# A gated delta rule layer: rows of decays reach all partitions by loads from memory instead of by matrix products

## The reference

```
gc = cumsum(g)                      # log decays, per head, inside a chunk of 64
dmat[i, j] = exp(gc[i] - gc[j])     # for j <= i, else 0
a_mat = strict_lower((k * beta) k^T * dmat)
qk    = lower(q k^T * dmat)
sol   = solve(I + a_mat, [v * beta, k * beta * exp(gc)])
q_dec = q * exp(gc)                 # queries that read the state
```

## Time and profile before

| | us |
|---|---|
| median of 3 runs (lowest, highest) | 1590.81 (1590.49, 1592.78) |
| the profiled execution, its own time | 1594.32 |
| its span in the trace | 1592.6 |
| PE busy | 1563.1 (98%) |
| PE weight loads busy | 1481.5 (93%) |
| DVE busy | 1055.5 (66%) |
| ACT busy | 884.4 (56%) |
| POOL busy | 256.2 (16%) |

### The profile page before, as it was taken

The page is one execution under the profiler, slowest core; times in us unless marked ns, Lnnn a source line. Parts: engine busy times, 40 slices in busy tenths (PEclk is TensorE's granted clock), DMA queues, the critical chain, the costliest instruction groups (busy, mean ns, idle before and its releaser), DMA issues.

```text
span 1592.6 us, 37769 instructions
## 1 busy us (share of the span) xinstructions
PE 1563.1 (98%) x16212; PEld 1481.5 (93%) x16212; DVE 1055.5 (66%) x1732; ACT 884.4 (56%) x1696; POOL 256.2 (16%) x328
## 2 busy tenths in 40 slices
PE   9999999999999999999999999999999999999997
PEld 7998799999997999999788888999999997999997
DVE  7965686755757877547793747776469837767643
ACT  6856656633645666434652546665358547566433
POOL 7105450000110200003003421100010035400000
PEclk9999999999999999999999999999999999999999
DMA  8941456565753665653635003665569512565550
GB/s 244 292 140 29 134 164 179 183 206 175 255 160 133 200 176 185 195 185 94 189 96 144 20 7 98 176 185 186 186 182 261 174 55 82 165 181 184 188 167 28
DMA packets 245529, 250.10 MB, mean 157 GB/s; under 512 B 16270, under 2 KB 239284, under 8 KB 245300
## 3 DMA queue, kind: packets, MB, share of 16 engines
q1 hardware_dynamic: 237204, 224.78, 46.3%
q0 software_dynamic: 8016, 22.86, 4.9%
q10 hardware_dynamic: 144, 0.05, 0.0%
HBM read 229.75 MB, written 18.32 MB: 156 GB/s over the span
## 4 chain that ended last, share of the span: by engine, by line
PE 92%; ACT 4%; DVE 3%; issue 1%; DMA 0%; SPq 0%; DVEq 0%
PE ps L844 88%; PE ps L848 4%; ACT vk L2053 1%; ACT tri L2053 1%; ACT acts L2053 1%; ACT st L2053 0%; DVE acts L2760 0%; ACT hn L2053 0%; DVE tri L2752 0%; DVE acts L2752 0%; DMA acts<-in_x_sample_dram 0%; ACT L2056 0%; PE ps L1796 0%; DVE st L2760 0%; DVE hn L2760 0%
## 5 line engine op out<-in xcount | busy, mean ns | idle before, releaser
L2752 DVE TENSOR_TENSOR w_mlp<-ring,w_mlp 128x1024 fp32r<-128x1024 f32 x256 | 311.7, 1224 | 119.9 <-ACT w_mlp L2053 113.9
L2053 ACT ACTIVATE w_mlp<-ring 128x1024 fp32r<-128x1024 f32 x256 | 269.4, 1054 | 208.2 <-PE ps L844 208.2
L844 PE MATMUL ps<-hn_split,w_mlp 128*128 128x264 f32 x3072 | 373.3, 284 | 0.0
L844 PE MATMUL ps<-h_split,w_mlp 128*128 128x264 f32 x3072 | 372.6, 283 | 0.0
L844 PEld LDWEIGHTS ps<-hn_split,w_mlp 128*128 128x128 f32 x3072 | 372.0, 188 | 0.3
L844 PEld LDWEIGHTS ps<-h_split,w_mlp 128*128 128x128 f32 x3072 | 371.6, 188 | 0.0
L2053 ACT ACTIVATE tri<-ps 128x264 f32<-128x264 f32 (+4 forms) x222 | 101.4, 463 | 181.2 <-PE ps L844 156.2
L844 PE MATMUL ps<-gdn_hi,w_gdn 128*128 128x264 f32 x896 | 165.8, 285 | 0.0
L844 PEld LDWEIGHTS ps<-gdn_hi,w_gdn 128*128 128x128 f32 x896 | 139.3, 188 | 0.9 <-issue 0.8
L844 PE MATMUL ps<-mixer_lo,w_gdn 128*128 128x264 f32 x448 | 126.9, 283 | 0.0
L2752 DVE TENSOR_TENSOR tri<-tri 128x264 f32<-128x264 f32 (+4 forms) x145 | 59.7, 413 | 101.3 <-ACT h_split L2053 100.6
(11 more groups left out here) (454 smaller groups left out, 2654.2 us busy)
## 6 DMA issues: line engine op xcount, KB each, us to landing
ring<-in_ffn_w_dram SPq DMA_DIRECT2D x128, 1024.0 KB, 5.4
ring<-in_gdn_w_in_dram SPq DMA_DIRECT2D x32, 1024.0 KB, 8.3
ring<-in_ml_w_in_dram SPq DMA_DIRECT2D x12, 1024.0 KB, 5.5
ring<-in_rw_w_rkv_dram SPq DMA_DIRECT2D x12, 1024.0 KB, 5.0
st<-in_state_gdn_S_dram POOLq DMA_DIRECT2D x2, 4096.0 KB, 22.4
ring<-in_gdn_w_out_dram SPq DMA_DIRECT2D x8, 1024.0 KB, 5.0
out_gdn_S_s_dram<-st SPq DMA_DIRECT2D x16, 512.0 KB, 6.8
st<-in_state_mlstm_C_dram POOLq DMA_DIRECT2D x1, 4096.0 KB, 20.5
```

The costliest lines, as they stand in the source:

```text
L844: return nc.tensor.matmul(out, lhsT, rhs, start=start, stop=stop)
L2053: return nc.scalar.activation(out, in_, f, bias=bias, scale=scale)
L2752: return nc.vector.tensor_tensor(out, in0, in1, op)
```

## The change

The products that spread rows over partitions are gone from both delta layers: the 32 of `spread` and the 8 of `spread_queries`. In their place one product of 16 output rows (8 heads of query exponents, 8 heads of matrix exponents) and 256 columns is made at the start of `decay_exponents` into bank 4. ACT copies these 16 rows to SBUF twice, once as they are and once as exponentials, and starts five DMAs from its own queue that write them to two small arrays in the chip's memory: 4 for the two matrices and the two groups of heads (16 runs of 256 bytes each), 1 for the queries (8 KB). POOL waits for all five (`row_out`) and starts three loads from there, whose source repeats the same 8 KB for every partition: two of 64 partitions x 8 KB into `AT6` and `QK6` at once, one of 128 partitions x 8 KB into `QS`. DVE waits for all three (`spr_in`), adds `negC` to each matrix with one operation in SBUF, and ACT takes both exponentials one after the other at n == 30. The exponentials of the queries are taken on the 16 rows, so the four ACT operations of 128x512 on `QS` are gone. The buffer of sample states `statio` moves to other space, which makes POOL clear it and `vv` ahead of `rtx` rather than after. In the constants the columns of `selt` are renumbered.

```diff
@@ names and arrays
-        qe_mm = rt_mm
-        spread_mm = kk_mm
+        row_mm = rt_mm
+        row_ev = rt_ok
+        exp_rows = [nc.dram_tensor(f"exp_rows{n}", (2, 2, 4, 4, HD), F32, kind="Internal").ap() for n in range(2)]
+        query_rows = [nc.dram_tensor(f"query_rows{n}", (GH, SEQ), F32, kind="Internal").ap() for n in range(2)]
+        row_log, row_exp = rows[0:2 * GH, 3, 0:SEQ], rows[0:2 * GH, 4, 0:SEQ]
-        statio = A(6).rearrange("p a b -> p (a b)")[:, 0:D].rearrange("p (h s n) -> p h s n", h=GH, s=NS)
+        statio = acts[:, 56:64, :].rearrange("p a b -> p (a b)")[:, 0:D].rearrange("p (h s n) -> p h s n", h=GH, s=NS)
@@ PE, decay_exponents, query_exponents and the fills
-                    for half in range(2):
-                        spread(0, 4 + half, half)
+                    b = 4
+                    pe.wait_ge(*last_read[b])
+                    mm(ps[b][0:2 * GH, 0:SEQ], selt[:, 0:2, :].rearrange("p a h -> p (a h)"), RG[:, 0:SEQ]).then_inc(row_mm, count.up(row_mm))
+                    last_read[b] = row_ev, count.seen(row_ev)
...
                 def query_exponents():
-                    for half in range(2):
-                        spread(4, 4 + half, half)
                     gram(0, 7)
                     gram(1, 6)
...
-                def spread_queries():
-                    for q in range(4):
-                        b = 2 + q
-                        pe.wait_ge(*last_read[b])
-                        for n in range(2):
-                            last = mm(ps[b][:, n * SEQ:(n + 1) * SEQ], sel(4, 2 * q + n, P), RG[:, 0:SEQ])
-                        last.then_inc(qe_mm, count.up(qe_mm))
-                        last_read[b] = eq_ev, count.expect(eq_ev)
...
-                fills = {(0, 0): sample_products, (0, 1): spread_queries, (1, 0): sample_outputs,
+                fills = {(0, 0): sample_products, (1, 0): sample_outputs,
@@ ACT
                     if n == 27:
+                        ac.wait_ge(row_mm, count.seen(row_mm))
+                        act(row_log, ps[4][0:2 * GH, 0:SEQ], ACT.Copy)
+                        act(row_exp, ps[4][0:2 * GH, 0:SEQ], ACT.Exp).then_inc(row_ev, count.up(row_ev))
+                        ac.wait_ge(row_ev, count.own(row_ev))
+                        for q in range(2):
+                            for g in range(2):
+                                at = q * GH + 4 * g
+                                ac.dma_start(exp_rows[j][g, q].rearrange("c h i -> h c i"),
+                                             rows[at:at + 4, 3, 0:SEQ].rearrange("h (c i) -> h c i", c=4)).then_inc(
+                                                 row_out, count.up(row_out, 16))
+                        ac.dma_start(query_rows[j], rows[0:GH, 4, 0:SEQ]).then_inc(row_out, count.up(row_out, 16))
                         ac.wait_ge(cols_mm, count.seen(cols_mm))
...
-                    if n in (29, 30):
-                        ac.wait_ge(da_ok, count.seen(da_ok, 2))
-                        part = AT6 if n == 29 else QK6
-                        act(part, part, ACT.Exp).then_inc(dt_ok, count.up(dt_ok))
+                    if n == 30:
+                        for part in (AT6, QK6):
+                            ac.wait_ge(da_ok, count.seen(da_ok))
+                            act(part, part, ACT.Exp).then_inc(dt_ok, count.up(dt_ok))
...
-                for q in range(4):
-                    ac.wait_ge(qe_mm, count.seen(qe_mm))
-                    act(QS[:, 2 * q:2 * q + 2, :], ps[2 + q][:].rearrange("p (n t) -> p n t", n=2), ACT.Exp).then_inc(
-                        eq_ev, count.up(eq_ev))
@@ DVE
-                dv.wait_ge(negc_ok, count.seen(negc_ok))
-                exponents(AT6, 4, 0)
-                exponents(AT6, 5, 1)
                 weight_lo()
+                dv.wait_ge(rtx_ok, count.seen(rtx_ok))
                 dv.wait_ge(cols_ok, count.seen(cols_ok))
...
-                exponents(QK6, 4, 0)
-                exponents(QK6, 5, 1)
+                dv.wait_ge(negc_ok, count.seen(negc_ok))
+                dv.wait_ge(spr_in, count.seen(spr_in, 48))
+                for part in (AT6, QK6):
+                    tt(part, part, negC, ALU.add).then_inc(da_ok, count.up(da_ok))
@@ POOL
-                gp_.tensor_tensor(hs8(rtx), bc(RG[:, SEQ:T], GH, 1), bc(mh[:], NS, 2), ALU.mult).then_inc(rtx_ok, count.up(rtx_ok))
                 gp_.memset(statio, 0.0)
                 gp_.memset(vv, 0.0)
+                gp_.tensor_tensor(hs8(rtx), bc(RG[:, SEQ:T], GH, 1), bc(mh[:], NS, 2), ALU.mult).then_inc(rtx_ok, count.up(rtx_ok))
+                count.seen(row_ev)
+                po.wait_ge(row_out, 80 * (j + 1))
+                for g, r in enumerate(halves):
+                    load(A(5).rearrange("p a b -> p (a b)")[r, 0:2 * D], bc(exp_rows[j][g].rearrange("s c h i -> (s c h i)"), HD, 0), spr_in)
+                load(QS.rearrange("p h t -> p (h t)"), bc(query_rows[j].rearrange("h t -> (h t)"), P, 0), spr_in)
                 po.wait_ge(cols_ok, count.seen(cols_ok))
...
-                        po.wait_ge(eq_ev, count.seen(eq_ev))
+                        if l == 1:
+                            po.wait_ge(spr_in, 48 * (j + 1))
```

26 lines of the change are left out of this document (6 added, 20 removed).

## The result

| | before | changed |
|---|---|---|
| median (lowest to highest) of 6 runs each, us | 1590.65 (1589.84 to 1593.66) | 1602.78 (1600.42 to 1608.86) |
| profiled execution, its span | 1594.32, 1592.6 | 1600.94, 1599.2 |

The changed kernel is slower: ratio 1.0078, 95% interval 1.0057 to 1.0099. That is 12.1 us in the medians and 6.6 in the two profiled executions. It lies 3.8 above the predicted range, on the side of the rival *the rows are back late*.

What follows compares the result with a forecast made beforehand. PE, busy 92% of the span, was taken to bound the kernel. Per layer +0.35 before level 0, -1.45 after it and +1.3 for the clock made +0.2, +0.4 in both: 1591.2 us, range 1584.5 to 1599.

Steps and rivals of the forecast that it cites:

- the rows are back late: Rival: rows land at 129, level 0 starts at 135.3, time 1596.6; chance 0.35 for late or more clock lost.
- landed to level 0: DVE's two adds, ACT's second exponential, Gram multiplications, a POOL mask and hand-overs before level 0: 6.3 us.
- PE's list: PE's products per delta layer: 7.25 us removed, 0.46 added, so 6.8 us go.
- ACT's copies and issues: After the row product: two copies of 0.3 to 0.45 us, five DMA issues of 0.4 each, last starting at 114.9.
- The store must land: From ACT's last issue until POOL goes on: 2.5 us, at 117.4 (116.2 to 119.3).
- The loads: Three loads of 2.1 MB ahead of level 0: 9.4 us (8.4 to 11.4), landed at 126.8.
- After level 0: Levels 1 and 2 of the solve: of 3.65 us removed, 1.45 remain per layer (bounds 2.8 and 0.7).
- the bank's wait: Level 1, half 0 waits for the bank that DVE reads, leaving 2.8 of 3.65 us.
- the masks beside `mvs`: POOL's level 2 masks meet DVE's masked values and run longer, giving back 1.35 us (0 to 2.1).
- The clock: PE's idle time of 3.3 us ahead of level 0 brings a clock fall: 1.3 us per layer (0 to 2.5).
- The sum: Both layers +0.4 us on the profiled 1594.32, less 3.5 for the median: 1591.2 (1581.5 best, 1602.9 worst).

Runs made afterwards that it cites:

- load_waits: Full change, but SP issues the next block's first weight load only when the three loads of the rows have landed; 1593.68 us, ratio 1.0015.
- split_and_waits: Full change, but DVE waits for the matrices' two loads alone and SP holds the next block's first weight load until these landed; 1586.23 us, ratio 0.9974.
- the second comparison: The full change run once more, unaltered, with a second profile, against the kernel before; 1600.96 us, ratio 1.0057.
- keep_busy: Full change plus eleven products that nobody reads on PE ahead of level 0; 1597.60 us, ratio 1.0042.
- with the masks ahead: Full change, DVE waiting for the matrices' loads alone, weight load held, POOL's masks ahead of the previous level's products; 1583.98 us, ratio 0.9953.
- split_wait: Full change, but DVE waits for the matrices' two loads alone and POOL waits for the query rows at level 1; 1594.21 us, ratio 1.0017.
- all_three: Full change with the matrices' loads made one onto 128 partitions, query rows awaited at level 1, weight load held; 1622.10 us, ratio 1.0198.
- queries_only: Kernel before, with only the query rows sent through memory and the matrices' products kept; 1593.44 us, ratio 1.0002.

## Why the prediction was wrong

In us, first layer:

| step | forecast | full change, first layer | without what lay across it |
|---|---|---|---|
| row product to last issue | 3.8 | 3.36 | 3.35 (load_waits) |
| last issue to landed | 2.5 (1.8 to 3.7 from rows) | 5.30 | 1.63 (load_waits) |
| loads landed | 9.4 (8.4 to 11.4) | 10.83 | 7.1 (split_and_waits, for the two that DVE needs) |
| landed to level 0 | 6.3 | 6.25 | 6.25 (load_waits) |
| in all | 22.0 | 25.74 | |

- *PE's list* (6.8 us gone, PE ready 18.7 after the row product): right. PE was through 18.73 after it.
- *ACT's copies and issues*, *landing to level 0*: right, to 0.4 and 0.05.
- *The store must land, 2.5*: the step that failed. It measured 5.30 and 5.27 in the two layers, outside its bounds of 1.8 to 3.7. It was sized from the medians of the earlier trace rows, without a look at what was in the queues beside them. For a store with nothing beside it 2.5 was even too much (1.63). The weight load that now comes at the same time was seen, and was put down as an argument for the late rival, with the answer that it is over before the big loads start. That is true and beside the point: it lies across the store, and everything behind waits for the last of five stores. 2.8 us.
- *The loads, 9.4*: 10.83 and 9.35 in the first profile, 10.99 and 10.82 in the second, so too small by 1.4 to 1.6 in three of four. The half rate on half the partitions, which the rule of the Trainium skill said (SBUF — State Buffer, section on the DMA port swizzle) and no row showed, is shown now. But what made 7.1 into 10.8 is DVE's wait for the query rows, which are not needed there. With the weight load away the three loads still took 9.61 and 11.19 (`load_waits`); why they vary stays open. The late rival named this place.
- *After level 0, 1.45 gained*: right, 1.65 (the bank's wait 0.99 for 0.85, the masks beside `mvs` as said). The order of POOL that avoids it was not thought of.
- *The clock, 1.3 with bounds 0 and 2.5*: mis-sized. In the four solves of the two profiles it cost 1.5, 1.5, 2.9 and 4.9 behind level 0; the last had a second fall, at 1326 to 1334. The price of one fall, 1.6, had been read right from the earlier trace rows; wrong was to count on less than one for each layer.
- *The sum*: the profile of before (1594.32) had falls of its own: at its start (its row product was at 111.12; at 109.58 in `load_waits`, whose granted clock was 1.00 there) and at 1344, 1.5 and 1.7 us. Taking 3.5 off for the median was right for before, but the changed kernel's median stands above its profile, not below.

The trace of before held the case of the failed step. Of the eight stores whose median of 1.8 is in the earlier trace rows, those issued from 463 to 465, with the engines all but idle, landed in 1.5; SP issued a weight load at 465.61, and the last store, at 466.7 and also of a few bytes, took 5.5. The store of 2 KB (3.7) had a weight load beside it too. From the windows 463 to 465, 465 to 466 and 467 to 468 of before:

```profile
out_m_s_dram<-rows POOLq DMA_DIRECT2D x4, 0.0 KB, 1.5
...
ring<-in_ml_w_out_dram SPq DMA_DIRECT2D x1, 1024.0 KB, 5.8
...
out_m_s_dram<-rows POOLq DMA_DIRECT2D x1, 0.0 KB, 5.5
```

So of the 12.1 us of the first comparison the trip is, by its profile, 4.1 + 2.6 ahead of level 0, less 3.3 behind it, 3.4 in all. By the profile of the second comparison it is 4.1 + 3.7 - 3.3 = 4.5 of 9.6. The rest, 8.7 and 5.1, is by difference the clock; it was not measured apart. The two profiles themselves show 3.0 and 7.8 of it in one execution each, and `keep_busy` lies 3.4 to 5.2 lower. How many falls a typical execution has can't be read, since a profile shows only one.

## What to carry to other kernels

Put rows on all partitions by loads only if the last byte lands before the consumer's other work is done; count what else is in the DMA queues between the store's issue and its landing, and wait for each load apart, at the place that needs it. With these two waits set right the same change is 5 us faster than before, and 7 with the masks ahead, not 12 slower. A wait of some microseconds on PE costs itself and then the clock: the forecast needs both. And size a transfer from single landings and what lay beside them, not from a median: here 1.5 and 5.5 stood behind one of 1.8.

## What the runs showed of the hardware that was not expected

- A store of 8 KB issued 0.6 us after a 1 MB weight load was landed 5.1 to 5.3 us after its issue (`split_wait`, the full change); with the load out of the way, 1.63. Stores of a few bytes in the kernel before: 1.5 alone, 5.5 beside such a load.
- A load whose outermost dimension is 2 uses two of the 16 engines: 1 MB landed after 23.9 us in `all_three` (49 GB/s), where 410 GB/s would be 2.6.
- The clock fell in the solve itself, with no wait or one of 0.32 us ahead of level 0 (`queries_only`, 0.50 and 0.66; `split_and_waits`, 3.5 us), in some layers and executions and not in others. PE was busy for 2.49 of the 4 us before the fall in `queries_only`, but for 2.50 of 4 from 152 to 156 in the full change too, where the clock stayed at 1.00. What decides stays open.
